# A hybrid decoder step: the input projection is moved ahead of everything and done by Strassen's seven products

## What is computed

```python
proj = rmsnorm(x, g_norm) @ w_in          # 1024 -> 10240 columns
u, z_p, q, k, v, z_r, gates = split(proj) # 1024,1024,1024,1024,2048,2048,2048
pooled = trailing means of u over 2/4/8/16 tokens, minus u
pooled = (pooled @ w_pool_group) * pool_scale                  # 4 groups of 256
y_pool = (pooled * silu(z_p)) @ w_branch_pool
o = retention(rope(q), rope(k), v)        # 4 heads, qk 256, v 512, chunked
y_ret = (groupnorm(o) * gn_ret * silu(z_r)) @ w_branch_ret
merged = sigmoid(gate_p) * y_pool + sigmoid(gate_r) * y_ret
y = rmsnorm(x + merged @ w_out) * g_final
```

## Time and profile before

| | us |
|---|---|
| median of three runs | 3252.88 |
| the three runs | 3252.42, 3252.88, 3256.05 |
| span of the profiled execution | 3250.7 |
| TensorE busy in it | 3164.1 |
| VectorE, ScalarE, GpSimd busy | 1673.2, 1053.1, 168.3 |

### The profile page before, as it was taken

One profiled execution on the slowest core, in us unless ns is written; L12 is line 12 of the kernel. 1 busy time (PEld: TensorE's weight loads), 2 busy tenths in 40 slices (PEclk: granted clock), 3 DMA queues, 4 the chain that ended last, 5 costly groups with the idle time before them and its releaser, 6 DMA issues.

```text
span 3250.7 us, 40799 instructions
## 1 busy us (share of the span) xinstructions
PE 3164.1 (97%) x13656; PEld 2444.9 (75%) x13656; DVE 1673.2 (51%) x2753; ACT 1053.1 (32%) x1670; POOL 168.3 (5%) x238
## 2 busy tenths in 40 slices
PE   7999999999999999999999999999999999999997
PEld 6888888888888888888888888888888888873222
DVE  4465554545555544545655554646556545534331
ACT  4233333443233323343333323443323223332210
POOL 2000000000000000000000000000000000001110
PEclk9999999999999999999999999999999999999999
DMA  5222323343222323333222323333322222349895
GB/s 164 88 78 83 98 78 91 101 147 124 81 87 74 98 80 91 124 132 113 88 87 68 103 82 93 124 127 110 94 85 77 87 91 88 119 165 328 286 312 191
DMA packets 232227, 384.98 MB, mean 118 GB/s; under 512 B 21608, under 2 KB 100712, under 8 KB 232063
## 3 DMA queue, kind: packets, MB, share of 16 engines
q1 hardware_dynamic: 212647, 318.91, 31.3%
q0 software_dynamic: 19456, 64.54, 5.6%
HBM read 347.39 MB, written 36.34 MB: 118 GB/s over the span
## 4 chain that ended last, share of the span: by engine, by line
issue 48%; PE 41%; DVE 6%; DMA 2%; POOL 2%; ACT 0%; POOLq 0%; DVEq 0%; ACTq 0%
PE bank L791 11%; PE bank L793 11%; PE bank L792 11%; PE bank L1043 6%; PE bank L1083 2%; DMA out_ret_prompt<-state 2%; DVE rot L1371 1%; DVE og L1371 1%; DVE ogt_lo L1499 1%; POOL inv_std L710 1%; PE bank L1076 1%; DVE state L1371 1%; DMA out_y_prompt<-xo 1%; DVE rot L1484 0%; POOL y L693 0%
## 5 line engine op out<-in xcount | busy, mean ns | idle before, releaser
L1371 DVE TENSOR_TENSOR w_lo<-raw,w_hi 128x512 fp32r<-128x512 f32 x934 | 623.4, 688 | 628.3 <-ACT w_hi L1135 626.5
L1135 ACT ACTIVATE w_hi<-raw 128x512 fp32r<-128x512 f32 x934 | 572.8, 632 | 1039.5 <-PE bank L793 1004.8
L791 PE MATMUL bank<-x_hi,w_hi 128*128 128x512 f32 x1536 | 598.5, 390 | 5.4 <-DVE x_lo L1398 4.4
L793 PE MATMUL bank<-x_hi,w_lo 128*128 128x512 f32 x1536 | 597.8, 389 | 0.0
L792 PE MATMUL bank<-x_lo,w_hi 128*128 128x512 f32 x1536 | 597.8, 389 | 0.0
L791 PE MATMUL bank<-w_hi,x_hi 128*128 128x512 f32 x1024 | 400.7, 391 | 0.5
L793 PE MATMUL bank<-w_hi,x_lo 128*128 128x512 f32 x1024 | 399.1, 390 | 0.0
L792 PE MATMUL bank<-w_lo,x_hi 128*128 128x512 f32 x1024 | 398.4, 389 | 0.0
L791 PEld LDWEIGHTS bank<-x_hi,w_hi 128*128 128x128 f32 x1536 | 288.3, 188 | 66.3 <-issue 6.1
L793 PEld LDWEIGHTS bank<-x_hi,w_lo 128*128 128x128 f32 x1536 | 288.3, 188 | 60.3
L792 PEld LDWEIGHTS bank<-x_lo,w_hi 128*128 128x128 f32 x1536 | 288.3, 188 | 60.3
(11 more groups left out here) (247 smaller groups left out, 3967.5 us busy)
## 6 DMA issues: line engine op xcount, KB each, us to landing
raw<-in_w_in SPq DMA_DIRECT2D x646, 256.0 KB, 2.7
raw<-in_w_branch_ret SPq DMA_DIRECT2D x128, 256.0 KB, 2.8
s_w<-in_w_in SPq DMA_DIRECT2D x64, 512.0 KB, 5.1
raw<-in_w_branch_pool SPq DMA_DIRECT2D x64, 256.0 KB, 3.0
raw<-in_w_out SPq DMA_DIRECT2D x64, 256.0 KB, 2.9
s_in<-in_state_ret SPq DMA_DIRECT2D x32, 512.0 KB, 8.8
out_ret_sample<-s_out POOLq DMA_DIRECT2D x32, 512.0 KB, 4.7
out_ret_prompt<-state POOLq DMA_DIRECT2D x20, 512.0 KB, 4.4
```

The lines of the kernel that those rows point to most:

```text
L791: pe.matmul(out, lh, rh, start=first, stop=False)
L793: return pe.matmul(out, ll, rh, start=False, stop=last)
L1135: act.activation(w_hi[:, n % RING, :], raw[:, n % RAW, :], ACT.Copy).then_inc(w_hi_done, 1)
L1371: return dve.tensor_tensor(out, a, b_, op).then_inc(s, 1)
```

## The change

The kernel is written anew in two parts with a border between them, without hardware loops in either.

The first part does the input projection alone. It goes over the tokens in NS = 2 halves of 1024. A half begins with a stage that makes its x operands (`x_parts` on ScalarE and VectorE, `inverse_x` on GpSimd, `x_transposes` on TensorE): four pairs of 128-token tiles through one buffer `xs`, each normalised, transposed, summed into Strassen's seven operands and split. Then 40 jobs of 256 columns follow. A job takes the 1024 x 256 weights as 2 x 2 quarters and the x as 2 x 2 quarters, and makes seven products of 4 x 3 = 12 matmuls in place of eight. GpSimd forms the four sums of weights, ScalarE and VectorE split seven operands of 128 x 512 and combine the products while they leave PSUM. Rotation, pooling windows and SiLU are done on the job's result (SiLU on GpSimd), k and v are transposed (16 transposes a job, woven into the next job), and all goes to tensors in HBM by SP.

The second part goes over 4 blocks of 512 tokens with what it loads back. A head loads q, k, v (2.5 MB) and z (1 MB), splits them (`head_high`, `head_low`), and the branch product of the head before it is woven between the chunks. The pooling and output products stand in a tail. The states stay on the chip. After the last block SP waits for all stores, and the sample tokens follow as before.

The sizes in bytes of the placement also change: `x` and `w` operands of the old projection both lie at multiples of 128 bytes, the old `ogt`, `pg` and `m` at 64 beyond one, and the new operands of each part all at one remainder (32 in the first part, 64 in the second).

```diff
+def job_list():
+    jobs = []
+    for h in range(HEADS):
+        v = [("v", h, 0), ("v", h, 1)]
+        z = [("z", h, 0), ("z", h, 1)]
+        g = [("gate", 2 * h, 0), ("gate", 2 * h + 1, 0)]
+        pool = [("zp", h, 0), ("u", h, 0)]
+        if h < HEADS - 1:
+            jobs += [("q", h, 0), g[0], ("k", h, 0), z[0], v[0], *pool, z[1], v[1], g[1]]
+        else:
+            jobs += [("q", h, 0), g[0], ("k", h, 0), z[0], v[0], v[1], *pool, z[1], g[1]]
+    return jobs
...
+            def x_rows(sb, p):
+                n = PAIRS * sb + p
+                if n:
+                    sp.wait_ge(x_turned, 4 * n)
+                if sb and p == 0:
+                    tab_free(sp, sb * NJ)
+                src = io["x_prompt"][0][sb * 2 * T:(sb + 1) * 2 * T, :].rearrange("(t i p) d -> p t i d", t=2, p=P)
+                sp.dma_start(xs[:], src[:, :, p, :]).then_inc(xs_in, 16)
...
+            for j in range(ALL):
+                if j + 2 < ALL:
+                    weights(j + 2)
+                if j + 1 == NJ:
+                    x_rows(1, 0)
+                    norm_row(1)
+                if j + 1 < ALL and (j + 1) % NJ and kind(j + 1) in ("q", "k"):
+                    rope_tables(j + 1)
+                if j:
+                    store(j - 1)
+                if j + 1 == NJ:
+                    for p in range(1, PAIRS):
+                        x_rows(1, p)
+                    rope_tables(j + 1)
+            store(ALL - 1)
...
+            def head_inputs(b, h):
+                hb = b * HEADS + h
+                s = hb % 2
+                if hb >= 2:
+                    sp.wait_ge(o_mm, 4 * (hb - 2) + 4)
+                if b and h < 2:
+                    sp.wait_ge(m_added, KT * b)
...
+            for b in range(NB):
+                for h in range(1, HEADS):
+                    for n in range((h - 1) * UH, h * UH):
+                        ahead(b, n)
+                    if h >= 2:
+                        pass
+                    if h + 1 < HEADS:
+                        head_inputs(b, h + 1)
+                        head_gates(b, h + 1)
+                sp.wait_ge(o_mm, 4 * (b * HEADS + 2) + 4)
...
+            sp.wait_ge(out_stored, 16 * NT * NB)
+            sp.wait_ge(state_stored, 16 * HEADS)
+            sp.wait_ge(out_squared, NT * NB)
+            unit_done(sp, NB * UB - 1)
...
+            def inverse_x(sb):
+                for p in range(PAIRS):
+                    n = PAIRS * sb + p
+                    pool.wait_ge(x_var_ready, n + 1)
+                    w = slice(2 * p, 2 * p + 2)
+                    pool.tensor_tensor(x_inv[:, w], x_var[:, w], half[:, 0:2], ALU.pow).then_inc(x_pow, 1)
...
+            def silu(j):
+                n = before(j, "z", "zp")
+                for t in range(2):
+                    pool.wait_ge(z_sig, 2 * n + t + 1)
+                    pool.tensor_tensor(c_out[:, j % 2, t], c_out[:, j % 2, t], tmp[t][:], ALU.mult).then_inc(z_mul, 1)
...
+            def one_product(j, i):
+                n = PROD * j + i
+                bank = banks[3 * (j % 2) + (0, 1, 0, 2, 0, 2, 0)[i]]
+                first = i in (A11B11, A12B21, S1T1)
+                pe.wait_ge(wa_lo_done, n + 1)
+                if i == A11B11 and j >= 2:
+                    pe.wait_ge(c21_done, j - 1)
+                if i == A12B21 and j >= 2:
+                    pe.wait_ge(c11_done, j - 1)
+                if i == S2T2:
+                    pe.wait_ge(s_copied, j + 1)
+                if i == S1T1 and j >= 2:
+                    pe.wait_ge(c12_done, j - 1)
+                if i == S3T3:
+                    pe.wait_ge(v_copied, j + 1)
+                if i == S4B22:
+                    pe.wait_ge(s5_copied, j + 1)
+                if i == A22T4:
+                    pe.wait_ge(c22_done, j + 1)
+                s = n % SLOTS
+                for k in range(KH):
+                    mm = split_product(bank[:], wa_hi[:, s, k, :], wa_lo[:, s, k, :], xa_hi[:, i, k, :],
+                                       xa_lo[:, i, k, :], first and k == 0, k == KH - 1, not first)
+                mm.then_inc(product, 1)
...
+            for j in range(ALL):
+                if j % NJ == 0:
+                    x_transposes(j // NJ)
+                    pe.wait_ge(x_lo_done, PROD * PAIRS * (j // NJ + 1))
+                    if j:
+                        pe.wait_ge(x_copied, 4 * PAIRS * (j // NJ + 1))
+                for i in range(PROD):
+                    one_product(j, i)
+                    if j and kind(j - 1) in ("k", "v") and 1 <= i < 5:
+                        turn(j - 1, i - 1)
...
+            def scores(hb, c):
+                s = hb % 2
+                pe.wait_ge(qk_lo_done, hb + 1)
+                if c == 0 and hb:
+                    pe.wait_ge(normed, 4 * hb)
...
+            def output(hb, c):
+                s = hb % 2
+                cross = c or hb >= HEADS
+                if cross:
+                    pe.wait_ge(st_lo_done, splits(hb, c) + 1)
+                pe.wait_ge(sc_lo_done, 2 * hb + c + 1)
+                if c:
+                    pe.wait_ge(normed, 4 * hb + 2)
...
+            def turn_og(hb):
+                if hb:
+                    pe.wait_ge(y_added, KT * hb)
...
+            def group(b, g):
+                n = GROUPS * b + g
+                outs = (0, 1) if g % 2 == 0 else (6, 7)
+                pe.wait_ge(pl_lo_done, n + 1)
...
+            for b in range(NB):
+                for h in range(HEADS):
+                    hb = b * HEADS + h
+                    scores(hb, 0)
+                    scores(hb, 1)
+                    if h:
+                        turn_og(hb - 1)
+                    update(hb, 0)
+                    output(hb, 0)
+                    if h:
+                        branch(hb - 1, 0)
+                    update(hb, 1)
+                    output(hb, 1)
+                    if h:
+                        branch(hb - 1, 1)
+                hb = b * HEADS + HEADS - 1
+                group(b, 0)
+                group(b, 1)
+                turn_og(hb)
+                branch(hb, 0)
+                group(b, 2)
+                group(b, 3)
+                branch(hb, 1)
+                branch_pool(b, 0)
+                branch_pool(b, 1)
+                project(b, 0)
+                project(b, 1)
+            pe.sem_inc(s_mm.sem, s_mm.credit)
...
+            def x_parts(sb):
+                for p in range(PAIRS):
+                    n = PAIRS * sb + p
+                    w = slice(2 * p, 2 * p + 2)
+                    dve.wait_ge(x_squared, 2 * n + 2)
+                    if n >= PAIRS:
+                        dve.wait_ge(x_normed, 2 * (n - PAIRS) + 2)
+                    dve.tensor_scalar(x_var[:, w], x_sum[:, w], 1.0 / D, EPS, ALU.mult, ALU.add).then_inc(x_var_ready, 1)
+                    dve.wait_ge(x_pow, n + 1)
+                    dve.wait_ge(norm_b_in, 16 * (sb + 1))
+                    for t in range(2):
+                        dve.scalar_tensor_tensor(out=xs[:, t, :], in0=xs[:, t, :], scalar=x_inv[:, 2 * p + t:2 * p + t + 1],
+                                                 in1=norm_b[:], op0=ALU.mult, op1=ALU.mult).then_inc(x_normed, 1)
...
+                    if n:
+                        dve.wait_ge(x_hi_done, PROD * n)
+                    dve.wait_ge(x_copied, 4 * n + 4)
+                    tt(x_s[:, 0], x_t[:, 2], x_t[:, 3], ALU.add, x_s_dve)
+                    dve.wait_ge(x_s_dve, 2 * n + 1)
+                    tt(x_s[:, 1], x_s[:, 0], x_t[:, 0], ALU.subtract, x_s_dve)
...
+            def mask_scores(hb, c):
+                dve.wait_ge(sc_mm, 2 * hb + c + 1)
+                if hb:
+                    dve.wait_ge(o_mm, 4 * hb)
+                if hb % HEADS == 0 and hb and c == 0:
+                    dve.wait_ge(out_stored, 16 * NT * (hb // HEADS))
...
+                    statistics(hb, 0)
+                    if h:
+                        lows(b, (h - 1) * UH, 1)
+                    output_bias(hb, 0)
+                    if h:
+                        lows(b, (h - 1) * UH + 1, 3)
+                        add_y(hb - 1, 0)
+                    if h + 1 < HEADS:
+                        head_low(hb + 1)
+                    new_state(hb, 1)
+                    statistics(hb, 1)
+                    if h:
+                        lows(b, (h - 1) * UH + 4, 1)
+                    output_bias(hb, 1)
+                    if h:
+                        lows(b, (h - 1) * UH + 5, 3)
+                    if b and h + 1 < HEADS:
```

2230 lines of the change are left out of this document (1181 added, 1049 removed).

## The result

The changed kernel takes 3423.4 us (median of 4 runs, 3420.5 to 3428.1), the kernel before 3252.7 (4 runs, 3250.9 to 3256.1): ratio 1.0521, 95% interval 1.0506 to 1.0536. It is slower by 171 us; the forecast had 3360, slower by 107, with a range of 3260 to 3455. The profiled execution has a span of 3421.3 us, to compare with the sum of 3359.

What follows compares the result with a forecast made beforehand. TensorE's issue was taken to bound the prompt part, transfers the sample tokens. Projection 1721, second part 1277, sample border 33.5 and the rest 327.7 sum to 3359, stated as 3360 us; own range 3300 to 3425, wider range 3260 to 3455.

Steps and rivals of the forecast that it cites:

- Start: Before the projection: loads, weight splits and four pairs of x through one buffer, 14.7 us a pair; first product at 79 us.
- Second x: Between the projection's halves: x operands made behind job 39, with TensorE idle for 62 us.
- Jobs: Projection's 80 jobs: matmuls 1524 us, transposes 46, and 10 of waits, mainly behind the pooling jobs.
- Rival (b): Projection jobs: VectorE and GpSimd shut each other out and set the jobs' length, 144 us more, 3504; chance 0.06.
- Heads of block 1: Second part, a block with a predecessor: 43.6, 44.2, 48 and 176.3 us, together 312, of which 49 idle.
- the clock: Second part: after gaps the granted clock falls to 1.2 GHz for a while, 5 us a block, from nothing to 12.
- Samples: Sample tokens: first panel 33.5 us after the last output product, then 327.7 us bound by transfers as before.
- Head 3 and the tail: End of a block in the second part: 162.6 us of matmuls and 13.7 idle, at `pooled_low`.
- The rule weighed: VectorE with two SBUF inputs and GpSimd reading SBUF exclude each other; 1.1 us a 512-column sum, unchanged by it.
- (a): Second part: gaps are filled, a block idles 20 us, 3224 in all; deciding point 27 us a block; chance 0.14.
- (c): All products: differing operand remainders of 128 bytes guessed slow; new placement slow everywhere, 84 us more, 3444; chance 0.12.
- (d): Whole kernel: matmuls are taken away but borders and gaps cancel them, 3250 +- 6; chance 0.03.

Runs made afterwards that it cites:

- experiment 5: Kernel after, with GpSimd's sums of weights in the projection on 8 columns instead of 512, leaving part of the computation out: 3405.3 us, ratio 1.0464.
- Experiment 1: Kernel after, with transfers of the next block's head 1 and head 0's gate issued behind the last fourteen weight units of w_out: 3396.0 us, ratio 1.0431.
- Experiment 3: Kernel after, with extra matmuls whose results nobody reads where TensorE would stand idle in the second part: 3426.4 us, ratio 1.0512.
- experiment 8: Kernel after, with the next head's q, k and v transfers issued ahead of the eight weight units in heads 1 and 2: 3357.8 us, ratio 1.0312.
- experiments 4 and 9: 4: kernel before, operand region 64 bytes later, 3239.4 us, ratio 0.9945. 9: kernel after, second part's split weights 64 bytes later, 3426.0 us, ratio 1.0523.
- the best version: Kernel after with five order and place edits, unread matmuls, pooling inputs split before y's gating, and x sums on VectorE: 3273.9 us, ratio 1.0051.

## Why the prediction was right, and where it was short

The direction and the main reason hold: matmuls go, and the borders, the second x stage and the idle time of the second part take more than they give. Step by step, forecast against the profiled execution:

- **Start**: first product at 79, measured 83.0. **Second x**: 62, measured 67.7; its period of 14.7 is 14.8. The first pair of the second stage begins 7.6 us after the last product instead of 11, but GpSimd's sums lengthen splits in each pair: two take 2.37 us, and the last pair's next four 5.68 and 6.75 in the two stages, where the other pairs have 2.48.
- **Jobs**: 1580 with stalls, measured 794.1 + 795.1 = 1589.2. A matmul costs 0.2267 in a stream. The stalls sit where they were put, at the pooling jobs, as 10.2 us of `part_s`. With experiment 5, GpSimd's part of projection and x stages is 18 to 23 us. A 512-column sum takes 1.27 us at the x stages and 1.31 to 1.62 among the jobs, for which 1.1 was taken. Rival (b) falls: it needed 144 us.
- **Border**: first scores at +21, measured +22.9; head 1's at +53, measured +54.5.
- **Heads of block 1**: head 0 43.6, measured 41.9; head 1 44.2, measured 49.7; head 2 48, measured 49.2; head 3 and tail 176.3, measured 190.3. The forecast of a block was 312 and 5 for the clock; blocks 1 and 2 took 331.1 and 331.0, block 3 320.3, block 0 from head 1 on 280.0 (forecast 268.5).
- **Samples**: first panel +33.5, measured +34.3; the rest 327.7, measured 330.2.

So 19 of the missing 62 us are in the projection, 40 in the second part, 3 behind it. In the second part one step failed and one term was too small. The step is "Head 3 and the tail: 162.6 of matmuls, 13.7 idle, at `pooled_low`": it has no wait at the output product, whose weights stand behind 7 MB for the next block. Experiment 1 prices it at 27 us, 9 a block. Block 3 has no next block, and is the one that is 11 us shorter. The term is the clock, 5 us a block within 0 to 12, against 16.0 beyond the full rate, 12.4 once the heads are in time. Experiment 3 adds a caution: removing it where VectorE sets the length gives nothing. The idle time of a block, 49 forecast and 52.0 measured, is near in its sum partly by luck. By head it was 25.7, 2.9, 6.7 and 13.7 in the forecast and 19.5, 5.9, 6.1 and 20.5 in block 1: head 0 waits less than forecast, and that covers most of the output product's 7.0 us. The heads' late inputs were worth more than the idle time they caused: experiment 8 took 13.5 us of idle time off a block and 3.6 us of half rate with it, since each pause also slows what follows and hands a late `y` to the next head. One reading ahead of the sum was wrong without harm: the costliest wait after the start is 8.8 us, in the sample part, and not 7.1.

**The rule weighed.** A VectorE split, with two inputs in SBUF, takes 833 ns in the mean beside GpSimd against 689 alone, the rotation step 2199 against 1225, and an instruction of 128x2 takes 1.26 us beside GpSimd's 1.27 against 0.16. The instruction with one input in PSUM (`c_out<-bank,part_s`) has a mean of 690 ns in both runs of experiment 5. By the page "SBUF — State Buffer" of the Trainium skill, section "Who interferes with whom", the two engines exclude each other on a shared pair of ports for a whole instruction; by that rule, the trace agrees, with the numbers above. The instruction of 128x2 has only one input in SBUF, so two inputs, the case that the prediction weighed, are not the only one that suffers. The prediction gave it no term of its own ("the sum would stay"), and it was about 20 us.

**Rivals.** (a) Filled gaps: 27 us a block was the point; the kernel as it is has 68, the best version 299.7 - 263.1 = 36.6, of which 12 are its unread matmuls, and it is still 0.5% over the kernel before. (c) The slow distance everywhere: none of it, the pooling product runs at 0.2267; the guess behind it is half right (experiments 4 and 9). (d) did not occur.

## What to carry to other kernels

Fewer matmuls pay only if every engine that prepared them has the time, at the borders too: here 198 us of issue were saved by the prediction's count, and start, second x stage, border, block heads and sample border, where one chain runs alone, cost more. When a block's work is reordered, write down for each transfer what stands ahead of it on its queue: two such orders (e1, e8) were worth 93 us, more than any other edit, and neither touched a computing instruction. A pause on TensorE costs its length and then some microseconds of half rate behind it, but only where TensorE is what the next step waits for.

## What the runs showed of the hardware

- In block 1, behind TensorE's pause of 8.94 us the first ten matmuls of 512 columns started 0.43 us apart (the very first 0.56); behind one of 3.92 us four started at the full rate and the next eight 0.39 to 0.43 apart; then it was 0.2267 again. In the second part of this kernel the granted clock was 0.93, with unread matmuls in the pauses 0.97.
- VectorE instructions took longer beside GpSimd's sums: 833 ns against 689 for a split of 512 columns, 2199 against 1225 for a rotation step of 1024, 4.49 us against 2.48 for two norms.
- The place of two operands relative to 128 bytes changed the distance of matmuls by 0.002 to 0.0066 us, 1 to 3%. In the kernel before that is 0.5% of the whole for an edit of one line. Why it is not the same in every product is open.
